# Recurrence of a first block: level products with whole 128x128 diagonal tiles as weights, masked on the way out of the bank

## The reference

```python
def wkv7_scan(r, decay, k, v, a, b, s0, reverse, return_y):
    # S_t = S_{t-1} (diag(w_t) + a_t b_t^T) + v_t k_t^T ;  y_t = S_t r_t
    def step(s, inp):
        rt, wt, kt, vt, at, bt = inp
        sa = jnp.einsum('bhvk,bhk->bhv', s, at)
        s = s * wt[:, :, None, :] + sa[..., None] * bt[:, :, None, :] + vt[..., None] * kt[:, :, None, :]
        y = jnp.einsum('bhvk,bhk->bhv', s, rt) if return_y else None
        return s, y
```

## Time and profile before

| | us |
|---|---|
| median of 3 runs | 3533.66 |
| lowest, highest | 3531.85, 3539.24 |
| the profiled execution, its own time | 3547.03 |
| its span in the profile | 3545.2 |
| PE busy in the span | 3214.5 |
| the recurrence's six steps | about 392 to 785 |

### The profile page before, as it was taken

How to read it: one execution, slowest core, us unless ns; L and a number is a source line. 1 busy time by engine, 2 the same in 40 slices (tenths; PEclk the granted TensorE clock), 3 DMA queues, 4 the chain that set the end, 5 groups by cost and what they waited for, 6 DMA issues and landing times.

```text
span 3545.2 us, 61398 instructions
## 1 busy us (share of the span) xinstructions
PE 3214.5 (91%) x26760; PEld 2565.7 (72%) x26760; DVE 1925.4 (54%) x2832; ACT 1255.5 (35%) x2068; POOL 171.8 (5%) x167
## 2 busy tenths in 40 slices
PE   6998788889798887699999799999999999899999
PEld 4866677775443333699888568998899887579997
DVE  3356665555321112788342748873887344658863
ACT  3226433331100000454232655443543333654432
POOL 0003221230100000000000000000000000000000
PEclk8989888899899999899999999999999999899999
DMA  6240000014599997232241012323232331013322
GB/s 229 72 143 22 2 3 3 3 35 179 222 383 421 421 421 322 85 108 93 104 148 66 13 60 72 108 96 131 72 108 96 131 113 60 1 60 94 104 94 83
DMA packets 174022, 441.53 MB, mean 125 GB/s; under 512 B 5954, under 2 KB 97852, under 8 KB 149180
## 3 DMA queue, kind: packets, MB, share of 16 engines
q1 hardware_dynamic: 173756, 437.61, 33.4%
HBM read 435.49 MB, written 2.10 MB: 123 GB/s over the span
## 4 chain that ended last, share of the span: by engine, by line
PE 68%; DVE 9%; DMA 7%; ACT 3%; issue 3%; SPq 0%; DVEq 0%; ACTq 0%
PE banks L338 8%; PE banks L3137 7%; PE banks L3140 7%; PE banks L3139 7%; PE banks L2309 6%; PE banks L3258 4%; PE banks L3259 4%; PE banks L3257 4%; DMA ring<-in_exp_w_gate 3%; DMA ring<-in_exp_w_up 2%; PE banks L1512 1%; PE banks L380 1%; DMA ring<-in_exp_w_down 1%; PE banks L334 1%; PE banks L1535 1%
## 5 line engine op out<-in xcount | busy, mean ns | idle before, releaser
L2309 PE MATMUL banks<-ring,arena 128*64 128x512 f32 x1120 | 265.7, 617 | 43.3 <-DMA ring<-in_exp_w_gate 19.5
L3259 PE MATMUL banks<-tail_r,hid_r 128*128 128x512 f32 x704 | 279.7, 397 | 0.0
L3258 PE MATMUL banks<-ring_r,two_r 128*128 128x512 f32 x640 | 254.0, 397 | 0.0
L3257 PE MATMUL banks<-tail_r,two_r 128*128 128x512 f32 x640 | 250.7, 392 | 0.0
L2309 PEld LDWEIGHTS banks<-ring,arena 128*64 128x64 f32 x1120 | 91.5, 142 | 204.3 <-issue 186.0
L3137 PE MATMUL banks<-ring_r,tail_r 128*128 128x256 f32 x624 | 175.6, 281 | 9.0 <-DVE arena L3222 9.0
L295 DVE TENSOR_TENSOR hid_r<-arena,two_r 128x1024 fp32r<-128x1024 f32 x40 | 49.0, 1226 | 238.1 <-ACT two_r L292 223.8
L3139 PE MATMUL banks<-ring_r,tail_r 128*128 128x256 f32 x624 | 175.9, 282 | 0.0
L3137 PE MATMUL banks<-mix_r,tail_r 128*128 128x256 f32 x624 | 175.5, 281 | 0.0
L3139 PE MATMUL banks<-h_r,tail_r 128*128 128x256 f32 x624 | 174.7, 280 | 0.0
L3140 PE MATMUL banks<-mix_r,ring_r 128*128 128x256 f32 x608 | 171.2, 282 | 0.0
(11 more groups left out here) (546 smaller groups left out, 8842.3 us busy)
## 6 DMA issues: line engine op xcount, KB each, us to landing
ring<-in_exp_w_gate SPq DMA_DIRECT2D x31, 2048.0 KB, 17.2
ring<-in_w_ffn_gate SPq DMA_DIRECT2D x44, 1024.0 KB, 5.4
ring<-in_w_ffn_up SPq DMA_DIRECT2D x44, 1024.0 KB, 5.4
ring<-in_exp_w_down SPq DMA_DIRECT2D x20, 2048.0 KB, 17.6
ring<-in_w_ffn_down SPq DMA_DIRECT2D x20, 2048.0 KB, 7.9
ring<-in_exp_w_up SPq DMA_DIRECT2D x19, 2048.0 KB, 16.2
ring<-in_w_in SPq DMA_DIRECT2D x17, 2048.0 KB, 10.2
arena<-in_exp_w_up SPq DMA_DIRECT2D x13, 2048.0 KB, 18.7
```

What stands on the lines that cost most here:

```text
L2309: ins = TE.matmul(banks[64 * e:64 * e + 64, b0 + hf, :], lhs(kk, e), w[:, k, hf * 512:(hf + 1) * 512], start=(kk == 0), stop=(kk == KD - 1))
L3257: TE.matmul(bank, h_hi, w_hi[:, c, ns], start=(f == 0), stop=False)
L3258: TE.matmul(bank, h_hi, w_lo[:, c, ns], start=False, stop=False)
L3259: ins = TE.matmul(bank, h_lo, w_hi[:, c, ns], start=False, stop=(f == NF - 1))
```

## The change

The first products of levels 1 to 4 no longer have masked 32 x 32 blocks as weights. A new tile `Abd` holds, for each of the 16 pieces, a 128 x 128 matrix with the unmasked 32 x 32 diagonal blocks of A, and zeros elsewhere. One product of 128 x 128 weights by 128 x 32 replaces four tiled ones. The level's mask is put on the result, which works since the mask selects entries by block: DVE multiplies it in while it takes the bank to `P1s`, with the other direction's mask. ACT's `p1` stays for the pairs alone.

`Abd` is filled by ACT (`diagonal`, quadrants 0 and 1) and by POOL (quadrants 2 and 3 from `Am32`), and its zeros are set once in `open_pool`. `Abd` takes the place of `Al`. `W_`, which shared `Al`'s memory, now shares that of `Xp` and `XTp`. On PE, level_p(1, 1) now comes ahead of gram(1). On DVE, the eight new instructions of a step stand among the masks and adds, and `w_dve` and `plus_dve` come ahead of add(2, 0) and add(3, 0).

```diff
-                Al = high.take(4, 16, 32)
+                Abd = high.take(16, P)
+                W_ = region(high.at, 2, 4, P)
...
+                lm_of_turned = lambda d, i: lm(1 - d, i)
...
                 def open_pool(l):
+                    l.did(G.memset(Abd, 0.0).then_inc(l.sem, 1))
...
                         def level_p(i, d):
-                            l.wait_ge(*past(co, "Al", i, d))
+                            if i == 1:
+                                l.wait_ge(*past(co, "Abd", d))
+                                l.wait_ge(*past(co, "Abd_high", d))
                             l.wait_ge(*past(co, "XT", i - 1, d))
...
                             for g in range(8 * d, 8 * d + 8):
-                                for b in range(4):
-                                    ins = TE.matmul(cols_of(lower(d), g)[quad(b)], Al[quad(b), i - 1, g, :], XTp[quad(b), g, :],
-                                                    start=True, stop=True, tile_position=(32 * b, 32 * b))
+                                ins = TE.matmul(cols_of(lower(d), g), Abd[:, g, :], XTp[:, g, :], start=True, stop=True)
...
                         level_p(1, 0)
+                        level_p(1, 1)
                         gram(1)
-                        level_p(1, 1)
...
+                        def diagonal(d):
+                            for b in (0, 1):
+                                l.did(S.activation(Abd[quad(b), 8 * d:8 * d + 8, quad(b)].rearrange("p (h j) n -> p h j n", h=2),
+                                                   banks[quad(b), 2 * d:2 * d + 2, :].rearrange("p h (j n) -> p h j n", j=4)[:, :, :, quad(b)],
+                                                   ACT.Copy).then_inc(l.sem, 1), co, "Abd", d)
...
                         pack(0)
+                        diagonal(0)
                         pack(1)
+                        diagonal(1)
                         whole(0)
-                        p1(1, 0)
                         whole(1)
-                        p1(1, 1)
-                        p1(2, 0)
-                        p1(2, 1)
...
+                        l.wait_ge(*l.own())
                         for d in range(2):
                             l.wait_ge(*past(sq_, "W_made", d))
...
+                        def p1(i, d):
+                            if n and i == 1:
+                                l.wait_ge(*past(before, "state", 1))
+                            l.wait_ge(*past(co, "P1_made", i, d))
+                            l.did(V.tensor_tensor(packed(P1s, d), of32(lower(d)), lm_of_turned(d, i), ALU.mult).then_inc(l.sem, 1),
+                                  co, "P1", i, d)
...
                         gm(0, 0)
+                        p1(1, 0)
                         gm(0, 1)
+                        p1(1, 1)
+                        gm(1, 0)
                         add(1, 0)
-                        gm(1, 0)
                         add(1, 1)
+                        p1(2, 0)
                         gm(1, 1)
-                        add(2, 0)
+                        p1(2, 1)
                         if more:
                             w_dve(l, n + 1, 0)
+                        add(2, 0)
                         add(2, 1)
                         gm(2, 0)
+                        p1(3, 0)
                         gm(2, 1)
+                        p1(3, 1)
...
-                        for i in LEVELS:
-                            for d in range(2):
-                                l.wait_ge(*past(co, "Am32", d))
-                                l.wait_ge(*past(co, "Am32_high", d))
-                                l.did(G.tensor_tensor(Al[:, i - 1, 8 * d:8 * d + 8, :], packed(Am32, d), lm(d, i), ALU.mult)
-                                      .then_inc(l.sem, 1), co, "Al", i, d)
+                        for d in range(2):
+                            l.wait_ge(*past(co, "Am32_high", d))
+                            for b in (2, 3):
+                                l.wait_ge(*l.own())
+                                l.did(G.tensor_copy(Abd[quad(b), 8 * d:8 * d + 8, quad(b)], packed(Am32, d)[quad(b)])
+                                      .then_inc(l.sem, 1), co, "Abd_high", d)
```

More of the change, by code:

```diff
@@ L1160, in part_three @@
                 U_ = region(RING * SLOT + 2 * P + 4 * T, 2, 4, P)
-                W_ = shaped(Al.rearrange("p a b c -> p (a b c)")[:, 0:2 * 4 * P], (2, 4, P))
                 P2s = Xp.rearrange("p g n -> p (g n)")
@@ L1466, in scaled_dve @@
                     l.did(V.tensor_tensor(ytm[:, t, :], ytm[:, t, :], fixed[:, t, :], ALU.add).then_inc(l.sem, 1), gn, "out", t)
-                LEVELS = (1, 2, 3, 4)
                 first = lambda d, b: 2 * b + d
@@ L1708, in whole, with p1 @@
                                       co, "Amf", d, h)
-                        def p1(i, d):
-                            l.wait_ge(*past(co, "P1_made", i, d))
-                            l.did(S.activation(packed(P1s, d), of32(lower(d)), ACT.Copy).then_inc(l.sem, 1), co, "P1", i, d)
+                        def p1(d):
+                            l.wait_ge(*past(co, "P1_made", 5, d))
+                            l.did(S.activation(packed(P1s, d), of32(lower(d)), ACT.Copy).then_inc(l.sem, 1), co, "P1", 5, d)
                         def spread(d, name, blocks):
@@ L1754, in step_act @@
                             gate_act(l, 0)
-                        p1(3, 0)
-                        p1(3, 1)
                         if more:
@@ L1760, in step_act @@
                             square_act(l, 1)
-                        p1(4, 0)
-                        p1(4, 1)
                         if more:
@@ L1768, in step_act @@
                             square_act(l, 2)
-                        p1(5, 0)
-                        p1(5, 1)
+                        p1(0)
+                        p1(1)
                         for d in range(2):
@@ L1860, in step_dve @@
                             mean_dve(l, 1)
-                        add(3, 0)
                         if more:
                             plus_dve(l, n + 1, 0)
+                        add(3, 0)
                         add(3, 1)
                         gm(3, 0)
+                        p1(4, 0)
                         gm(3, 1)
+                        p1(4, 1)
                         if more:
```

## The result

The changed kernel takes 3584.72 us (median of 4 runs, 3560.01 to 3611.78). The kernel before took 3535.59 in the runs beside it (4 runs, 3531.85 to 3539.24). The ratio is 1.0129, with a 95% interval of 1.0099 to 1.0159: slower by 49 us. The change costs what the sum said. The four runs of the changed kernel spread over 52 us, those of before over 7; that by itself says little, since 21 later runs of before spread over 29 us and four later ones of the changed kernel over 18.

The account below looks back on a forecast made before the run. PE (91% busy) was taken as the bound, with instruction stops and a lowered clock. Terms +44.4, -36.5, +6.6, -5.8 and +39.4 sum to +48.1 us on 3533.7, giving 3581.8 us, range 3526 to 3610.

Parts of the forecast that it names:

- First products: level_p on PE: 768 full-width passes at 111.5 ns, 85.6 us, replace 3072 small ones busy 41.2 us; +44.4 us.
- Fewer instructions: PE's instruction stream in the six steps: 2304 passes go, so all stops for instructions go; -36.5 us, bounds -49.6 and 0.
- The clock: PE's level passes: thin columns lower the granted clock, half of 768 passes run at the lower level; +39.4 us, bounds 0 and +78.7.
- +8.7: Whole change: the forecast sum left when the clock term goes, in us.
- gram(1) behind: PE order: moved behind level_p(1,1), gram(1) leaves a gap open and adds its own 1.1 us; +6.6 us over six steps.
- Waits covered: PE's 11.6 us wait for DVE before cum_pe: longer levels should cover half; -5.8 us, bounds 0 and -11.6.
- Masking on DVE, POOL's copies, ACT's copies: Masked evictions on DVE (20 us), block copies on POOL and ACT: hidden in idle time or harmless, adding nothing.
- The clock stays up: Rival, PE clock: the clock term goes and slow work gets quick, -4 to -17 us, about 3523; chance 0.15.
- One replaces the other: Rival, PE levels: clock as now or slightly better, longer passes only fill the former stops, 3527 to 3541 us; chance 0.13.
- The stops are not the instruction supply: Rival, PE issue stops: they stay because instruction fetching is mostly hidden, 3618 us; chance 0.05.
- The clock did come back within the levels: Answers the rival that PE's clock never comes back within the levels, all 768 passes slow, +87.5, 3621 us; chance 0.13.
- PE waited for no P1 of the DVE: Answers the rival on DVE's order: every P1 waits behind a mask, +33 us, 3575 or 3614 us; chance 0.07.

Follow-up runs that it names:

- e6: Kernel before with only quadrant 0 of each level's first product made (768 passes of 32x32, not 3072), eviction scaled by 0; 0.9908, 3512.5 us beside 3545.2.
- e3: Changed kernel with before's 32x32 tiles on unmasked blocks of A, without Abd and POOL's masks, DVE masking kept; 1.0000, 3550.2 us beside 3549.1.
- e8: The changed kernel itself measured once more, nothing altered, for its spread; 1.0151 of the kernel before, 3601.4 us beside 3545.2.
- e4: Changed kernel with 64 moving columns instead of 32 in seven of eight level products, the added ones unused; 1.0011, 3553.9 us beside 3549.1.
- e1: Changed kernel with gram(1) moved back between level_p(1,0) and level_p(1,1); 1.0119 of the kernel before, 3593.4 us beside 3549.1.
- e2: Kernel before with gram(1) moved behind level_p(1,1), nothing else; 1.0004, 3545.8 us beside 3545.2.
- e5: Changed kernel with each first product made as two 64x64 tiles instead of one 128x128, 1536 passes in all; 0.9935, 3527.7 us beside 3549.1.
- e7: Changed kernel with two 64x64 tiles per first product and 64 moving columns in seven of eight pieces; 0.9911, 3514.9 us beside 3545.2.

## Why the prediction was right

*First products.* The pitch was right: 109 to 113 ns at the upper clock, 215 at the lower, at 16, 32 and 64 columns alike. +44.4 stands.

*Fewer instructions.* Right. -36.5 was foretold, and of these 36.5 us 1.7 are left. Over the stage PE's idle time fell by 40.9. e6 shows the cause by taking the passes away alone, e3 by putting them back (28.3 us of issue again), and the stops' places in the instruction list show it directly.

*The clock.* The decisive term, right in size and partly wrong in its working. I put half of the 768 passes at the lower level. By their start times 208 of them, 27%, ran there: 208 x 0.1025 = 21 us and not 39.4. (In e8 it was 242.) What I left out is the other work that the same fall slows: the 85.9 us of new busy time are 70.9 in the first products (112.1 - 41.2) and 15.0 in all the rest. 21 + 15 = 36. Two errors nearly cancelled, and that is luck. (The first products are 26.5 above their +44.4, 5 more than the 21: about what the last pass of each of 30 groups takes beyond the pitch, 0.28 against 0.11 us, an estimate.) By line the 15 us lie in cum_pe, in_pe, the grams and the joins (pair and whole), and none in the W, U, S and Y products, as foretold; that all of it is the clock's is argued from this and not shown alone.

e4, with the long passes and less of the fall, is the check on the whole term. The changed kernel is 42 to 50 us slower than e4. But e4 is also better off than the kernel before, with 77 us at the lower level against 94. Against the kernel before, the changed one has 68 to 95 us more there, at 0.45 us each some 31 to 43 us, where the sum has 39.4; the rest of the change is then e4's +4 and 17 x 0.45, some +12, where the sum has +8.7. These are estimates: e4's interval alone is 12 us wide.

*gram(1) behind.* +6.6 is not shown; e1 and e2 see nothing at either side, and an effect of that size would be inside their intervals.

*Waits covered.* Here the reading of the rows was wrong. Of the 11.6 us, 7.6 are a wait ahead of the six steps, which longer levels can't cover and which stays in the changed kernel (6.9 us, in e8 7.4). Only 4.0 us were there to win, and both profiles of the changed kernel win nearly all of them: -3.7 and -4.0, where -5.8 was foretold.

*Masking on DVE, POOL's copies, ACT's copies.* Nothing foretold. e3 finds nothing for the masks; for the copies there are only the waits above.

*The rivals.* "The clock stays up" did not happen. It is the rival to which the Trainium skill's rule led (TensorE: Matmul & The Clock Gate, Why this matters for your kernels: keep the engine continuously busy). The profile disagrees for thin passes: PE is busy 93% of the six steps after the change against 83% before, and its clock is lower. "One replaces the other" needed the clock of before, and e4, which has somewhat more than that, lands there (1.0011): the clock is what decides between that rival and the forecast. "The stops are not the instruction supply" falls by e6, by e3 and by the packets' times. So the trace does not agree that such fetching is mostly hidden (the Trainium skill, Runtime: NRT & Kernel Launch, Instruction fetch mechanics) where 32x32 passes come this thick: it held PE up for 36.5 us here. The clock did come back within the levels: 560 of the 768 passes ran at the upper one. And PE waited for no P1 of the DVE.

That the sum met the median within 1 us is luck beyond this: the terms for gram(1) and for the covered waits are not what they were taken for, and the changed kernel measured again gave 1.0151, 53 us.

What stays open: why a run has 162 or 190 us at the lower level. The time of a run goes with its clock; no run here steers it.

## What to carry to other kernels

Before wide weights replace packed small tiles, price the pass by its weight load and then ask what the thinner stream of columns does to the granted clock: a busy engine can lose its clock, as here with PE busy 93% of the stage at 0.82. Where a stream of tiny passes shows regular "issue" gaps one instruction packet apart, fewer passes pay, but try the tile size between the two: here 64x64 won 0.7 to 0.9% (e5, e7) where 128x128 lost 1.3%. If a pass is bound by its weights, more columns cost nothing (109 and 113 ns for 32 and 64), and even useless ones can pay: with them the clock was 0.91 for 0.82, and the kernel 42 us faster.

## What the runs showed of the hardware that was not expected

More work was faster, at the same number of passes: 64 columns gave 1.0011 where 32 gave 1.0129 and 1.0151. Less work was at least not faster: 16 columns gave 1.0174.

A 32x32 pass is cheap only beside its neighbours. In e6 768 passes in a single quadrant are busy 38.6 us, nearly the 41.2 us of 3072 passes in four. The timeline of e6 has two calls at the lower clock and two at the upper:

```profile
406.05 1.91 PE L1524 MATMUL banks<-arena 32*32 32x32 f32 x32
414.35 1.19 PE L1524 MATMUL banks<-arena 32*32 32x32 f32 x32
```

At the upper clock that is 1.19 / 32 = 37 ns a pass, where four quadrants in turn took 1.40 / 128 = 11 (532.09 in the earlier trace rows). Part of the likeness of the two sums is the clock: 406 of the 768 passes of e6 ran at the lower level, 1152 of the 3072 before. e6's gain is hence not in the products' own time. It is idle time: 395 - 348.0 = 47 us, where the kernel before had 72.7.
